# Hybrid attention/mLSTM block on one core: earlier parameter transposition, eight places for token tiles, row scales turned by VectorE, convolution in two halves

## The chip, the cores and the metric

One Trainium2 chip, one of its cores; one launch of one kernel. The metric is device time in microseconds (us) of that core. All engines of the core work side by side and meet at semaphores: TensorE (PE), VectorE (DVE), ScalarE (ACT), GpSimd (POOL), and SyncE (SP), which here only issues transfers.

## The reference, cut to what matters

Everything is float32. The input `x` is 1024 tokens by 1024 features. What bears on the change is the head of the block:

```python
h = rms_norm(x, g_mix[l])
p = h @ w_in[l]
aq, ak, av, mq, mk, mv, mo, mi, mf = jnp.split(p, split_idx, axis=-1)
...
qk = jax.nn.silu(causal_dwconv(jnp.concatenate([mq, mk], axis=-1), conv_qk[l]))
gates = jnp.concatenate([mi, mf], axis=-1).astype(jnp.float32) + b_gates[l].astype(jnp.float32)
...
mix = jnp.concatenate([rms_norm(att, g_attn_out[l]), rms_norm(mh, g_mlstm_out[l])], axis=-1)
x = x + mix @ w_out[l]
h2 = rms_norm(x, g_ffn[l])
x = x + (jax.nn.silu(h2 @ w_gate[l]) * (h2 @ w_up[l])) @ w_down[l]
```

`rms_norm` divides each token by the root of its mean square (the row scale) and multiplies by a gain per feature. `causal_dwconv` is a filter of four taps along the tokens on the 512 columns `mq, mk`. Windowed attention (eight heads) and a chunkwise mLSTM (four heads) stand between the two quoted pieces.

## The kernel before, in words

**Arithmetic.** Each float32 product is made of three matmuls of split operands: high by high, high by low, low by high (`three`, L829 to L835). A high part is written by ACT (`x_high`, `w0_high`, `w_high`) or, from the third weight group on, by POOL; the low part by DVE (`x_low`, `w0_low`) or POOL (`split`, L694).

**Order of the work.** Every engine runs a list that is written out by hand in its own block (`sync`, `gpsimd`, `tensor`, `scalar`, `vector`); what an engine's queue reaches late, everything behind it reaches late too.

1. `mq_half(0)` and `mq_half(1)` (L875 to L895) compute the 512 columns `mq, mk` in transposed form, features on partitions, for tokens 0 to 511 and 512 to 1023. Each half takes K = 8 blocks of 128 features, 12 matmuls each, into four banks: banks 0 to 3 in the first half, 4 to 7 in the second. `x_cols` is a transposed copy of x; its first half and the weights `w0_raw` come in as eight pairs of transfers (L556, L557), the second half as two transfers of 1 MB (`load_x_second`).
2. Units U = 8 to 55 (`unit`, then `out_unit`) work on one tile of 128 tokens each, eight units to a group (T = 8). Group 1 (U = 8 to 15) is 264 columns wide: keys, values and gates. Group 2 is the mLSTM values, 3 its output gate, 4 the queries, 5 and 6 the output projection. Units alternate between banks 0 and 1. Between the units small matmuls of the recurrence stand; the first of them, two products of `lf` with `tri` and `ones` (L1083, L1084), comes after unit U = 2T+2 = 18.
3. The feed-forward part: products of seven forms per quadrant from a fast 2 by 2 block scheme, with weight blocks streamed in by SP, split by ACT and POOL. It fills the time from about 380 us to the end and is not touched.

**Row scales.** They are not in the transposed product, so a scale per token is needed along the free axis. ACT squares and sums the eight token tiles `x_in` (`square_sum`, L1304), four at a time, and makes `rstd`, one column per tile (`row_scales`). `rstd` is stored to memory as a row of 512 numbers (`rstd_rows`), each of its elements a piece of its own, and SP loads that row into all partitions (`load_rstd`, L585). `mq_rows(b)` on DVE (L1710) multiplies half b by it on the way from the banks to `rawT`. Until `mq_rows(0)` has emptied two banks, unit U = 8 can't start (`mq_evac`). The four places of `x_in` are filled twice (`load_x`, L549).

**Parameters.** SP loads ten small pieces after the eight pairs (L558 to L568): the triangle `tri`, the rows of `prow` (convolution taps and gains), gate biases and sinks. PE transposes `prow` between the two halves (L1072) into bank 7; DVE copies the result to `cols` (L1813 to L1815) after all of its `x_low` work, and only then may PE write bank 7 again: `pe.wait_ge(gains_ready, 2)` stands before the fourth matmul of `mq_half(1)`.

**Convolution.** `convolution(f)` (L1774, L1776) handles 128 features by 1024 tokens in four passes of DVE; the four f run in U = 9 to 12 of DVE's list, after `mq_rows(1)`. ACT applies the SiLU to `qkT` f by f at U = 12, 14, 16 and 17 (L1451). Behind the convolution, DVE's list has U = 16: squares and sums of keys, gates (`absf`), and at U = 17 `lf` (L1857), which needs two small ACT steps (L1466, L1467) in between.

Of the kernel before, what the change touches and what calls it, by code (L numbers as in the profile page):

```python
# [29 lines left out]
ALU = mybir.AluOpType  # L30
# [43 lines left out]
def hymba_block(nc, x, g_mix, w_in, b_gates, conv_qk, q_gain, k_gain, sinks,  # L74
# [22 lines left out]
    x_t = x.rearrange("a (t p) d -> t p (a d)", p=P)  # L97
    out_t = out.rearrange("a (t p) d -> t p (a d)", p=P)
# [8 lines left out]
    with ctx:  # L107
# [64 lines left out]
        w0_raw, j_end = place("w0_raw", [P, K, N], at=J)  # L172
        ksq, _ = place("ksq", [P, T, P], at=J)
# [43 lines left out]
        grow, e = place("grow", [K, P], at=e)  # L217
        x_in = [x_in0, x_in1, x_in2, x_in3]
# [60 lines left out]
        rstd_s = sem("rstd_rows_loaded")  # L279
        w1_s = sem("w1_loaded")  # L280
# [264 lines left out]
        def _(sp):  # L545
            def load_x(t):
                if t >= 4:
                    sp.wait_ge(x_sq, t - 3)
                sp.dma_start(x_in[t % 4][:, :], x_t[t]).then_inc(x_in_s[t % 4], 16)  # L549
# [14 lines left out]
            for half in range(2):
                sp.dma_start(prow[G_K:G_K + 1, half * HD:(half + 1) * HD], k_gain).then_inc(par_s, 16)
                sp.dma_start(prow[G_Q:G_Q + 1, half * HD:(half + 1) * HD], q_gain).then_inc(par_s, 16)
            sp.dma_start(bias_g[:, :], b_gates[0:1, :].to_broadcast([P, 8])).then_inc(par_s, 16)
            sp.dma_start(sinks8[:, :], sinks[0:1, :].to_broadcast([P, 8])).then_inc(par_s, 16)  # L568
# [1662 lines left out]
```

## Time and profile before

| | |
|---|---|
| median of 3 runs | 1000.84 us (1000.76 to 1000.9) |
| profiled execution, its own time | 1005.44 us |
| its span | 1003.7 us |
| PE busy | 991.8 us (99%) |
| DVE, ACT, POOL busy | 635.1, 422.7, 668.4 us |
| moved by DMA | 70.69 MB |

The span is the stretch from the first to the last recorded instruction; the execution's own time holds it and a little around it. Busy time of PE counts matmuls with modelled ends, so 99% says that PE is almost always occupied, not how fast its clock runs; the granted clock (1.0 is full) stands in a column of its own in the view of stretches. A row of the timeline gives start, duration, engine, line, operation and tiles, and in brackets how long the engine had been idle and what ended that. SPq and ACTq are the queues that issue transfers.

### The profile page before, as it was taken

The page shows a single profiled execution, that of the slowest core. Times are in us where ns is not written, and L with a number is a line of the kernel's source. Part 1 is how long each engine was busy: PE and PEld are TensorE (multiplying, and loading weights), DVE is VectorE, ACT ScalarE, POOL GpSimd, SP SyncE. Part 2 cuts the span into 40 slices and gives each one's busy share as a digit, 9 for nine tenths or more (in the row PEclk, how much of TensorE's full clock was granted, in tenths as well). Part 3 has the DMA queues.
Part 4 walks back from the last instruction along what each step waited for, and adds up shares of the span by engine and source line. Part 5 has one row for each costly group of instructions (what it writes and reads, how often), then busy time and mean ns, then how long its engine had stood idle before and what let it go on. Part 6 is the DMA issues. An engine that isn't in the chain of part 4 may idle for free.

```text
span 1003.7 us, 13162 instructions
## 1 busy us (share of the span) xinstructions
PE 991.8 (99%) x4862; PEld 822.5 (82%) x4862; DVE 635.1 (63%) x777; ACT 422.7 (42%) x868; POOL 668.4 (67%) x529
## 2 busy tenths in 40 slices
PE   9899999999999999999999999999999999999998
PEld 7697788888888888888888888888888888888887
DVE  5259224558862677876748577774748586674585
ACT  6533135547750657524334352434334252433440
POOL 0238056726675516996887786887878788787792
PEclk9999999999999999999999999999999999999999
DMA  8823112141032002112112112112112112211213
GB/s 307 190 75 104 42 43 64 54 147 33 23 126 63 22 11 74 53 42 84 43 42 84 42 43 85 43 42 77 50 42 70 57 42 60 67 42 49 82 59 137
DMA packets 74423, 70.69 MB, mean 70 GB/s; under 512 B 6520, under 2 KB 54776, under 8 KB 74360
## 3 DMA queue, kind: packets, MB, share of 16 engines
q1 hardware_dynamic: 72296, 69.36, 22.6%
q10 hardware_dynamic: 2064, 0.50, 0.3%
q8 instruction: 39, 0.64, 0.3%
q14 instruction: 24, 0.20, 0.1%
HBM read 65.14 MB, written 4.21 MB: 69 GB/s over the span
## 4 chain that ended last, share of the span: by engine, by line
PE 87%; DVE 5%; DMA 3%; SPq 3%; ACT 1%; issue 1%; DVEq 0%; ACTq 0%
PE banks L833 27%; PE banks L835 27%; PE banks L834 27%; DVE qkT L1776 2%; DMA x_in<-in_x 1%; SPq L577 1%; DMA rstd_rows<-rstd 1%; PE banks L1030 1%; PE banks L846 1%; PE banks L927 1%; PE banks L1005 1%; DVE qkT L1774 1%; ACT prob L1541 1%; PE banks L992 1%; DMA rstd_b<-rstd_rows 1%
## 5 line engine op out<-in xcount | busy, mean ns | idle before, releaser
L763 POOL TENSOR_TENSOR wr_lo<-wr_raw,wr_hi 128x512 fp32r<-128x512 f32 x231 | 319.1, 1412 | 27.3 <-ACT wr_hi L1356 22.2
L757 POOL TENSOR_TENSOR wr_raw<-wr_raw,wr_raw 128x512 f32<-128x512 f32 x132 | 193.4, 1469 | 132.2 <-PE banks L835 75.8
L833 PE MATMUL banks<-hf_hi,wr_hi 128*128 128x512 f32 x616 | 240.2, 390 | 0.0
L835 PE MATMUL banks<-hf_hi,wr_lo 128*128 128x512 f32 x616 | 240.0, 390 | 0.0
L834 PE MATMUL banks<-hf_lo,wr_hi 128*128 128x512 f32 x616 | 239.9, 389 | 0.0
L1356 ACT ACTIVATE wr_hi<-wr_raw 128x512 fp32r<-128x512 f32 x231 | 136.7, 625 | 164.8 <-POOL wr_raw L757 107.7
L2177 DVE TENSOR_TENSOR x<-banks,x 128x1024 f32<-128x1024 f32 x138 | 168.8, 1224 | 51.5 <-PE banks L835 35.2
L833 PE MATMUL banks<-w_hi,actT_hi 128*128 128x512 f32 (+1 forms) x384 | 147.9, 385 | 0.0
L835 PE MATMUL banks<-w_hi,actT_lo 128*128 128x512 f32 (+1 forms) x384 | 144.2, 375 | 0.0
L834 PE MATMUL banks<-w_lo,actT_hi 128*128 128x512 f32 (+1 forms) x384 | 144.1, 375 | 0.0
L833 PEld LDWEIGHTS banks<-hf_hi,wr_hi 128*128 128x128 f32 x616 | 115.7, 188 | 24.3 <-issue 0.4
L835 PEld LDWEIGHTS banks<-hf_hi,wr_lo 128*128 128x128 f32 x616 | 115.7, 188 | 24.1
L834 PEld LDWEIGHTS banks<-hf_lo,wr_hi 128*128 128x128 f32 x616 | 115.7, 188 | 23.8
L833 PE MATMUL banks<-wr_hi,af_hi 128*128 128x512 f32 x308 | 120.0, 390 | 0.2 <-DVE x L2177 0.2
L834 PE MATMUL banks<-wr_lo,af_hi 128*128 128x512 f32 x308 | 120.0, 389 | 0.0
L835 PE MATMUL banks<-wr_hi,af_lo 128*128 128x512 f32 x300 | 116.8, 389 | 0.0
L2071 DVE TENSOR_TENSOR af_raw<-banks,af_raw 128x512 f32<-128x512 f32 x33 | 22.8, 691 | 128.9 <-PE banks L835 128.9
L694 POOL TENSOR_TENSOR w_lo<-w_raw,w_hi 128x512 fp32r<-128x512 f32 (+1 forms) x48 | 62.3, 1303 | 61.5 <-ACT w_hi L1372 58.9
L2095 DVE TENSOR_TENSOR af_lo<-af_raw,af_hi 128x512 fp32r<-128x512 f32 x75 | 88.8, 1226 | 0.3
L833 PEld LDWEIGHTS banks<-w_hi,actT_hi 128*128 128x128 f32 x384 | 72.9, 190 | 13.4 <-issue 1.4
L835 PEld LDWEIGHTS banks<-w_hi,actT_lo 128*128 128x128 f32 x384 | 72.8, 190 | 13.1
L834 PEld LDWEIGHTS banks<-w_lo,actT_hi 128*128 128x128 f32 x384 | 73.0, 190 | 11.6
(205 smaller groups left out, 1201.4 us busy)
## 6 DMA issues: line engine op xcount, KB each, us to landing
wr_raw<-in_w_up SPq DMA_DIRECT2D x46, 256.0 KB, 3.4
wr_raw<-in_w_gate SPq DMA_DIRECT2D x44, 256.0 KB, 3.3
wr_raw<-in_w_down SPq DMA_DIRECT2D x44, 256.0 KB, 3.2
w_raw<-in_w_in SPq DMA_DIRECT2D x32, 256.0 KB, 3.6
x_in<-in_x SPq DMA_DIRECT2D x8, 512.0 KB, 11.6
w_raw<-in_w_out SPq DMA_DIRECT2D x16, 256.0 KB, 2.6
x<-in_x SPq DMA_DIRECT2D x8, 512.0 KB, 5.6
out<-x SPq DMA_DIRECT2D x16, 256.0 KB, 2.1
```

The lines of the kernel that those rows point to most:

```text
L577: sp.dma_start(w1_raw[:, k, a:b], src).then_inc(w1_s, 16)
L694: nc.gpsimd.tensor_tensor(w_lo[:, ring, 0:width], w, w_hi[:, ring, 0:width].bitcast(F32), ALU.subtract).then_inc(w_ready, 1)
L757: nc.gpsimd.tensor_tensor(wr_raw[slot(q, f)][:, :], wr_raw[slot(q, a)][:, :], wr_raw[slot(q, b)][:, :], ALU.subtract).then_inc(wsum, 1)
L763: nc.gpsimd.tensor_tensor(wr_lo[s][:, :], wr_raw[s][:, :], wr_hi[s][:, :].bitcast(F32), ALU.subtract).then_inc(wf_lo, 1)
L833: nc.tensor.matmul(ps, x_hi, wh, start=first, stop=False, skip_group_check=more)
L834: nc.tensor.matmul(ps, x_hi, wl, start=False, stop=False, skip_group_check=more)
L835: return nc.tensor.matmul(ps, x_lo, wh, start=False, stop=last, skip_group_check=more)
L1356: nc.scalar.activation(wr_hi[s][:, :], wr_raw[s][:, :], ACT.Copy).then_inc(wf_hi, 1)
L1776: ins = V_.scalar_tensor_tensor(y, rawT[:, f, i:i + S], cols[:, 4 * i + f:4 * i + f + 1], y, ALU.mult, ALU.add)
L2071: V_.tensor_tensor(dst[:, :], src[:, :], dst[:, :], ALU.add).then_inc(added, 1)
L2095: V_.tensor_tensor(af_lo[b][f][:, :], af_raw[b][f][:, :], af_hi[b][f][:, :].bitcast(F32), ALU.subtract).then_inc(act_lo_s, 1)
L2177: V_.tensor_tensor(xs, banks[first + h][:, :, :], xs, ALU.add).then_inc(down_add, 1)
```

## The change

- The ten parameter loads of SP stand after the fourth of the eight pairs, not after the eighth.
- PE transposes `prow` inside `mq_half(0)`, before its block k = 6; DVE copies it to `cols` before its `x_low(1, k)` work.
- `x_in` has eight places (four tiles of two): the last four lie on `w0_raw`, which is dead once the first half's weights are split (`w0_ready`). Loads take two tiles each. The loads of `w1_raw` come after all of x, as two transfers in place of sixteen.
- DVE copies the four columns of `rstd` into a 32-wide tile and transposes it in blocks of 32 by 32 (`turn_scales`); ACT stores the turned rows in four transfers of four pieces of 128 bytes (`store_rows`) and ACT, not SP, loads the row back (`load_rows`).
- ACT's list: the squares of the second four tiles come before the splitting of group 1's weights, and `store_rows(1)` stands in the middle of the latter.
- The convolution is cut by tokens: 16 passes of 512 on the first half before `mq_rows(1)`, 16 on the second half after it, in place of 16 passes of 1024.

```diff
@@ layout
-        x_in0, e = place("x_in0", [P, D], at=E)
-        x_in1, e = place("x_in1", [P, D], at=e)
-        x_in2, e = place("x_in2", [P, D], at=e)
-        x_in3, e = place("x_in3", [P, D], at=e)
+        x_in0, e = place("x_in0", [P, 2, D], at=E)
+        x_in1, e = place("x_in1", [P, 2, D], at=e)
...
+        x_in2, _ = place("x_in2", [P, 2, D], at=J)
+        x_in3, _ = place("x_in3", [P, 2, D], at=J + 8 * D)
+        rpad, e = place("rpad", [P, 2, 32], at=e)
+        rpadT, e = place("rpadT", [P, 2, 32], at=e)
@@ sync
-            def load_x(t):
-                if t >= 4:
-                    sp.wait_ge(x_sq, t - 3)
-                sp.dma_start(x_in[t % 4][:, :], x_t[t]).then_inc(x_in_s[t % 4], 16)
+            def load_x(i):
+                sp.dma_start(x_in[i][:, :, :], x_p[:, 2 * i:2 * i + 2, :]).then_inc(x_in_s[i], 16)
...
-            for t in range(4):
-                load_x(t)
+            load_x(0)
+            load_x(1)
             load_x_second(1)
-            for k in range(K):
-                for (a, b), src in slice_source(k):
-                    sp.dma_start(w1_raw[:, k, a:b], src).then_inc(w1_s, 16)
-            for t in range(4, T):
-                load_x(t)
...
-            load_rstd(0)
+            sp.wait_ge(w0_ready, K)
+            load_x(2)
+            load_x(3)
+            sp.dma_start(w1_raw[:, :, 0:8], w_in_p[:, :, GATES:GATES + 8]).then_inc(w1_s, 16)
+            sp.dma_start(w1_raw[:, :, 8:NKV], w_in_p[:, :, AK:AK + 2 * KV * HD]).then_inc(w1_s, 16)
@@ tensor, mq_half
+                    if (b, k) == (0, 6):
+                        pe.wait_ge(gains_ready, 1)
+                        pe.wait_ge(par_s, 16 * PARAMS)
+                        nc.tensor.transpose(bank[7][:, 0:G_ROWS], prow[:, :],
+                                            ident[0:G_ROWS, 0:G_ROWS]).then_inc(gains_tp, 1)
@@ scalar
-                act.dma_start(rstd_dram[b:b + 1, :].rearrange("a (t p) -> p (a t)", p=P),
-                              rstd[:, tt], allow_slow_non_contiguous=True).then_inc(rows_stored, 16)
+            def store_rows(b):
+                act.wait_ge(rstd_turned, b + 1)
...
+                rows = rstd_dram[b:b + 1, :].rearrange("a (t q j) -> q (a t) j", q=4, j=32)
+                for q in range(4):
+                    act.dma_start(rows[q], rpadT[32 * q:32 * q + 4, b, :]).then_inc(rows_stored, 16)
+            def load_rows(b):
+                act.wait_ge(rows_stored, 16 * 4 * (b + 1))
+                act.dma_start(rstd_b[:, b * H:(b + 1) * H],
+                              rstd_dram[b:b + 1, :].to_broadcast([P, H])).then_inc(rstd_s, 16)
...
+            load_rows(0)
             for t in range(4, T):
                 square_sum(t)
             row_scales(1)
+            for n in range(4):
+                w_high(n)
+            store_rows(1)
+            for n in range(4, K):
+                w_high(n)
+            load_rows(1)
@@ vector
+            def turn_scales(b):
+                dve.wait_ge(rstd_ready, b + 1)
+                link(V_.tensor_copy(rpad[:, b, 0:4], rstd[:, 4 * b:4 * b + 4]))
+                V_.transpose(rpadT[:, b, :], rpad[:, b, :]).then_inc(rstd_turned, 1)
...
+            for k in range(4):
+                x_low(1, k)
+            turn_scales(0)
+            for k in range(4, K):
+                x_low(1, k)
             mq_rows(0)
+            dve.wait_ge(mq_evac, 4)
+            dve.wait_ge(x_sq, 4)
+            convolution(0, 0)
+            turn_scales(1)
+            for f in range(1, 4):
+                convolution(f, 0)
```

ACT's list from the first row scales on, before (L1315 is the store of `rstd`, L1326 `x_high`, L1372 `w_high`, L1304 a tile's squares):

```order
L1295 ACTIVATE rstd<-stat,cols 128x4
L1296 ACTIVATE rstd<-rstd 128x4
L1315 DMA rstd_rows<-rstd 128x4x1
L1326 ACTIVATE actT_hi<-actT_raw,cols 128x512 x4
L1372 ACTIVATE w_hi<-w_raw 128x264 x8
L1304 ACTIVATE junk,stat<-x_in_118 128x1024
L1304 ACTIVATE junk,stat<-x_in_119 128x1024
L1304 ACTIVATE junk,stat<-x_in_120 128x1024
L1304 ACTIVATE junk,stat<-x_in_121 128x1024
```

The same place of ACT's list now (L1312 is `store_rows`, L1316 `load_rows`, L1296 the squares, L1373 `w_high`):

```order
L1288 ACTIVATE rstd<-rstd 128x4
L1312 DMA rstd_rows<-rpadT 4x32 x4
L1327 ACTIVATE actT_hi<-actT_raw,cols 128x512 x4
L1316 DMA rstd_b<-rstd_rows 128x512
L1296 ACTIVATE junk,stat<-x_in_94 128x1024 x2
L1296 ACTIVATE junk,stat<-x_in_95 128x1024 x2
L1287 ACTIVATE rstd<-stat,cols 128x4
L1288 ACTIVATE rstd<-rstd 128x4
L1373 ACTIVATE w_hi<-w_raw 128x264 x4
L1312 DMA rstd_rows<-rpadT 4x32 x4
L1373 ACTIVATE w_hi<-w_raw 128x264 x4
L1316 DMA rstd_b<-rstd_rows 128x512
```

The squares moved ahead of the eight weight slices, and the second store now splits these slices four and four; each store waits for DVE's transposition, each load for the stores.

DVE's list from its second `x_low` series on, before (L1701 is `x_low`, L1813 and L1815 write `cols`, L1710 is `mq_rows`):

```order
L1701 SCALAR_TENSOR_TENSOR actT_lo<-actT_raw,cols,actT_hi 128x512 x8
L1813 COPY cols<-banks 128x26
L1815 TENSOR_SCALAR cols<-cols 128x1
L1823 COPY sink_b<-sinks_60 64x8 x2
L1825 TENSOR_SCALAR nsink<-sink_b 128x8
L1710 TENSOR_TENSOR rawT<-banks,rstd_b 128x512 x8
L1834 TENSOR_SCALAR nrstd<-rstd 128x8
L1837 MEMSET mvx 128x32
L1774 TENSOR_SCALAR qkT<-rawT,cols 128x1024
L1776 SCALAR_TENSOR_TENSOR qkT<-rawT,cols,qkT 128x1024 x3
```

DVE's list there now, from the copy to `cols` (L1824) on:

```order
L1824 COPY cols<-banks 128x26
L1826 TENSOR_SCALAR cols<-cols 128x1
L1834 COPY sink_b<-sinks_60 64x8 x2
L1836 TENSOR_SCALAR nsink<-sink_b 128x8
L1704 SCALAR_TENSOR_TENSOR actT_lo<-actT_raw,cols,actT_hi 128x512 x4
L1776 COPY rpad<-rstd 128x4
L1777 STREAM_TRANSPOSE rpadT<-rpad 128x32
L1704 SCALAR_TENSOR_TENSOR actT_lo<-actT_raw,cols,actT_hi 128x512 x4
L1713 TENSOR_TENSOR rawT<-banks,rstd_b 128x512 x4
L1782 TENSOR_SCALAR qkT<-rawT,cols 128x512
L1784 SCALAR_TENSOR_TENSOR qkT<-rawT,cols,qkT 128x512 x3
L1776 COPY rpad<-rstd 128x4
```

The copy to `cols` moved ahead of the eight `x_low`; `mq_rows` was one series of eight and is now four, the first convolution piece and the second turn, with the other pieces behind.

SP's list after the two large transfers of `x_cols`, before (L577 loads `w1_raw`, sixteen in all, of which the last two stand here; L549 is the second filling of `x_in`, L585 `load_rstd`):

```order
L577 DMA w_raw<-in_w_in 128x8
L577 DMA w_raw<-in_w_in 128x256
L549 DMA x_in_118<-in_x 128x1024
L549 DMA x_in_119<-in_x 128x1024
L549 DMA x_in_120<-in_x 128x1024
L549 DMA x_in_121<-in_x 128x1024
L585 DMA rstd_b<-rstd_rows 128x512
L613 DMA w_raw<-in_w_in 128x512 x2
L585 DMA rstd_b<-rstd_rows 128x512
L613 DMA w_raw<-in_w_in 128x512 x14
```

SP's list there now:

```order
L552 DMA x_in_120<-in_x 128x2x1024
L552 DMA x_in_121<-in_x 128x2x1024
L555 DMA actT_raw<-x_cols 128x4x512
L552 DMA x_in_94<-in_x 128x2x1024
L552 DMA x_in_95<-in_x 128x2x1024
L580 DMA w_raw<-in_w_in 128x8x8
L581 DMA w_raw<-in_w_in 128x8x256
L604 DMA w_raw<-in_w_in 128x512 x16
```

All of x is asked for before `w1_raw`, and neither load of the row scales is in SP's list any more.

## Rows read from the trace of the kernel before

**Rows 1.** Waits of PE: who for whom, us in total, times, longest.
```profile
PE banks L883 <- DVE cols L1815: 4.2, 1, 4.2
PE banks L1083 <- DVE lf L1857: 2.3, 1, 2.3
```

**Rows 2.** Timeline of PE around the two halves.
```profile
5.73 1.17 PE L883 MATMUL banks<-actT_hi,w_hi 128*128 128x512 f32 x4 [0.34 <-ACT w_hi L1360]
...
27.87 0.97 PE L883 MATMUL banks<-actT_hi,w_hi 128*128 128x512 f32 x3
33.03 0.80 PE L883 MATMUL banks<-actT_hi,w_hi 128*128 128x512 f32 x1 [4.19 <-DVE cols L1815]
...
54.71 1.07 PE L892 MATMUL banks<-actT_hi,w_lo 128*128 128x512 f32 x4
55.62 0.28 PE L833 MATMUL banks<-w_hi,actT_hi 128*128 128x264 f32 x1
```

**Rows 3.** Stretches with PE's busy time and granted clock, behind each long wait.
```profile
32.60:36.00 3.40, 2.97 (x7) 0.50 0.74 23
97.40:104.20 6.80, 6.73 (x18) 0.50 0.15 46
```

**Rows 4.** Timeline of PE around unit 19.
```profile
94.75 0.39 PE L835 MATMUL banks<-w_hi,actT_lo 128*128 128x512 f32 x1
97.47 0.64 PE L1083 MATMUL banks<-lf,tri 128*128 128x32 f32 x2 [2.33 <-DVE lf L1857]
...
98.35 0.78 PE L833 MATMUL banks<-w_hi,actT_hi 128*128 128x512 f32 x1
...
106.65 0.27 PE L1088 MATMUL banks<-ident,u 128*32 128x128 f32 x1
```

**Rows 5.** Timeline of DVE, 60 to 98 us.
```profile
60.74 2.48 DVE L1710 TENSOR_TENSOR rawT<-banks,rstd_b 128x512 f32<-128x512 f32 x4 [12.24 <-DMA rstd_b<-rstd_rows]
...
96.63 0.79 DVE L1857 SCALAR_TENSOR_TENSOR lf<-gate,expf 128x32 f32<-128x32 f32 x1 [0.56 <-ACT expf L1467]
```

**Rows 6.** Timeline of ACT, 20 to 97 us.
```profile
20.03 1.34 ACT L1326 ACTIVATE actT_hi<-actT_raw,cols 128x512 fp32r<-128x512 f32 x2 [3.33 <-DMA actT_raw<-x_cols]
...
28.21 0.40 ACTq L1315 DMA_DIRECT2D rstd_rows<-rstd  x1
...
89.74 0.69 ACT L1412 ACTIVATE mvx<-banks,rstd 128x512 f32<-128x512 f32 x1 [3.80 <-PE banks L835]
91.43 1.06 ACT L1451 ACTIVATE qkT<-qkT 128x1024 f32<-128x1024 f32 x1 [1.00 <-DVE qkT L1776]
92.51 1.28 ACT L1453 ACT_TABLE_LOAD   x1
94.92 0.31 ACT L1295 ACTIVATE krs<-kss,cols 128x16 f32<-128x16 f32 x1 [1.13 <-DVE kss L1847]
```

**Rows 7.** Timeline of SP's queue: issue of transfers.
```profile
9.13 0.45 SPq L558 DMA_DIRECT2D tri<-consts  x1
...
12.88 0.43 SPq L552 DMA_DIRECT2D actT_raw<-x_cols  x1
```

**Rows 8.** Stretches: ACT's busy time, PE clock, DMA share, GB/s.
```profile
14.00:17.00 3.00, 2.49 (x4) 1.00 0.56 117
...
30.00:39.00 9.00, 2.56 (x6) 0.81 1.03 68
```

**Rows 9.** Issues of transfers, 0 to 120 us: KB each, median us to landing.
```profile
rstd_rows<-rstd ACTq DMA_DIRECT2D x2, 2.0 KB, 9.0
nm_rows<-nM SPq DMA_DIRECT2D x1, 16.0 KB, 1.4
```

**Rows 10.** The row scales' way back into SBUF (`rstd_b`), both loads.
```profile
DMA to landing us min/median/max: 5.1/6.7/8.2
```

**Rows 11.** Timeline of POOL: the low parts of group 1's eight slices.
```profile
38.70 5.76 POOL L694 TENSOR_TENSOR w_lo<-w_raw,w_hi 128x264 fp32r<-128x264 f32 x8 [36.91 <-ACT w_hi L1372]
```

**Rows 12.** The line of the convolution on DVE: ns min/median/max.
```profile
L1776 DVE SCALAR_TENSOR_TENSOR qkT<-rawT,cols,qkT x12: 1284/1567/2415, 64.7 to 89.9; 128x1024 f32<-128x1024 f32 x12
```

More of the change, by code:

```diff
@@ L564, in _ @@
[L564 to L568, printed above, removed]
+                if k == 3:
+                    sp.dma_start(tri[:, :], consts[:, C_TRI:C_TRI + P]).then_inc(par_s, 16)
+                    sp.dma_start(prow[G_CONV:G_CONV + 16, :],
+                                 conv_qk.rearrange("a i (f p) -> (a i f) p", p=P)).then_inc(par_s, 16)
+                    for i, g in enumerate((g_att, g_ml)):
+                        rows = slice(G_OUT + 4 * i, G_OUT + 4 * i + 4)
+                        sp.dma_start(prow[rows, :], g.rearrange("a (k p) -> (a k) p", p=P)).then_inc(par_s, 16)
+                    for half in range(2):
+                        sp.dma_start(prow[G_K:G_K + 1, half * HD:(half + 1) * HD], k_gain).then_inc(par_s, 16)
+                        sp.dma_start(prow[G_Q:G_Q + 1, half * HD:(half + 1) * HD], q_gain).then_inc(par_s, 16)
+                    sp.dma_start(bias_g[:, :], b_gates[0:1, :].to_broadcast([P, 8])).then_inc(par_s, 16)
+                    sp.dma_start(sinks8[:, :], sinks[0:1, :].to_broadcast([P, 8])).then_inc(par_s, 16)
@@ L1069, in _ @@
             mq_half(0)
-            pe.wait_ge(gains_ready, 1)
-            pe.wait_ge(par_s, 16 * PARAMS)
-            nc.tensor.transpose(bank[7][:, 0:G_ROWS], prow[:, :],
-                                ident[0:G_ROWS, 0:G_ROWS]).then_inc(gains_tp, 1)
             mq_half(1)
@@ L1380, in _ @@
             act.wait_ge(ones_set, 2)
-            x_high(1, 0)
-            x_high(1, 1)
-            square_sum(0)
-            square_sum(1)
-            x_high(1, 2)
-            x_high(1, 3)
-            square_sum(2)
-            square_sum(3)
+            for k in range(4):
+                x_high(1, k)
+            for t in range(4):
+                square_sum(t)
             row_scales(0)
+            store_rows(0)
             for k in range(4, K):
                 x_high(1, k)
-            for n in range(K):
-                w_high(n)
+            load_rows(0)
             for t in range(4, T):
@@ L1767, in _, with convolution @@
                 w0_low(k)
[L1768 to L1774 removed]
+            def turn_scales(b):
+                dve.wait_ge(rstd_ready, b + 1)
+                link(V_.tensor_copy(rpad[:, b, 0:4], rstd[:, 4 * b:4 * b + 4]))
+                V_.transpose(rpadT[:, b, :], rpad[:, b, :]).then_inc(rstd_turned, 1)
+            def convolution(f, b):
+                y = qkT[:, f, b * H:(b + 1) * H]
+                link(V_.tensor_scalar(y, rawT[:, f, b * H:(b + 1) * H], cols[:, f:f + 1], None, ALU.mult))
                 for i in range(1, TAPS):
[L1776 to L1777 removed]
+                    ins = V_.scalar_tensor_tensor(y, rawT[:, f, b * H + i:b * H + i + H],
+                                                  cols[:, 4 * i + f:4 * i + f + 1], y, ALU.mult, ALU.add)
                     if i < TAPS - 1:
                         link(ins)
[L1780 removed]
+                    elif b == 0:
+                        step(ins)
+                    else:
+                        ins.then_inc(conv_ready, 1)
             def query_stats(t):
@@ L1838, in _ @@
                 if T + 1 <= U < T + 5:
-                    convolution(U - T - 1)
+                    convolution(U - T - 1, 1)
                 if U == 2 * T:
```

37 lines of the change are left out of this document (10 added, 27 removed).

## The prediction

> **What bounds the kernel now.** I read the busy table first: PE is busy 991.8 of 1003.7 us, so only what keeps PE waiting, or slows its clock, can be won. The waits of PE come next. Two stand out: 4.2 us for DVE's `cols`, 2.3 us for DVE's `lf` [rows 1]. The timeline shows what each cost.
>
> First seam. Four matmuls take 0.91 us (54.71 to 55.62). A half has 24 such fours, 21.8 us. The second half starts at 27.87, would end at 49.63 and ends at 55.62 [rows 2]. That is **6.0 us**: 4.5 of standing still (27.87 plus three matmuls is 28.55, the next one starts at 33.03) and 1.5 because the granted clock behind the wait is 0.50, the lower of the two levels, 1.2 GHz, until 36.0 [rows 3]. The missing thing is `gains_ready`: DVE copies `cols` behind its last four `x_low`, these need the last transfer of `x_cols`, and `cols` itself needs neither.
>
> Second seam. After the last matmul of unit 18 at 94.75 PE would go on at 94.98; it starts at 97.47, runs its two small products in 0.88 and unit 19 up to 106.65, and the clock is 0.50 for 6.8 us [rows 3, 4]. At the full clock the small ones take 0.44 and unit 19 takes 24 x 0.227 = 5.44, so PE would be through at 100.86: **5.8 us**. The chain of waits names the reason: row scales land, `mq_rows(1)` starts only at 60.74 after 12.2 us of idling, then come 27 us of convolution (passes from 64.7 to past 89.9) and 5 us of sums, and `lf` starts at 96.63 [rows 5, 12].
>
> Both waits are at the head. Behind unit 19 only waits of 0.4 us and less remain up to the last stage, and the later queues are paced by PE, so what the head saves moves everything forward.
>
> **The change, part by part.**
>
> *Parameters and `cols`.* The transposition moves from between the halves into the first, same cost. `gains_ready` comes about 1 us after PE's block 6, near 23 us, and PE asks for it at 28.5. The wait goes, with the low clock: -6.0. The price is SP's queue: ten issues between 9.13 and 12.88 [rows 7] now stand ahead of pairs 5 to 8, which are asked for 3.75 us later. Near 14 to 17 us the transfers dropped to 117 GB/s [rows 8]; I read that as these small pieces and move the hole to about 9 to 12. Pair 5 is then in near 13. PE needs block 4 at 5.73 + 4 x 2.72 = 16.6, and ACT at most 1.4 before that (two steps take 1.34 [rows 6]): 2 us of cover, and more for each later pair, since 2.72 us of PE stand against 1.3 of transfer. Cost nothing; if the cover is gone, PE waits for block 4. The large transfer behind keeps its place in the queue (issued at 12.88, in at 20.0 [rows 6, 7]). DVE's copies (0.9 us) delay its first `x_low(1, k)` to about 24; PE wants it at 28.8.
>
> *Row scales.* They are ready at 28.2, as before [rows 6]. Turning takes two small DVE operations, 0.5. Four issues of 0.4 end at 30.4. Then the store has to land. Before, 512 pieces of 4 bytes took 9.0 us; the only other store of rows, 32 pieces of 512 bytes, took 1.4 [rows 9]. Those are the bounds; for 16 pieces of 128 bytes I take 2, by the number of pieces, in which the new one is nearer to the fast row. ACT's four `x_high` (2.7) stand between, so `load_rows(0)` goes out at 33.1. It landed in 5.1 to 8.2 us before [rows 10]; the 8.2 fell into 30 to 39 us, where transfers crawled at 68 GB/s while the 4-byte pieces were under way [rows 8]. I take 5.1, so the scales are in at L = 38.4 (46.0 before). PE needs two banks emptied at 49.63: L + 1.3. Covered by 10 us.
>
> *The new queueing on ACT.* `store_rows(1)` waits for the second turn, which on DVE stands behind `mq_rows(0)` (2.5 us [rows 5]) and the first convolution piece. Behind the store on ACT are the last four slices of group 1's weights, and PE waits for those. A pass of 1024 took 1.28 to 2.42 [rows 12], so four passes of 512 cost 2.6 to 4.8; I take 3.2, since POOL is half idle there. Then 0.5 for the turn, 1.6 for the issues, and two slice steps of at most 0.72 each, ACT's and POOL's [rows 11]: slice 4 is ready at L + 9.2 = 47.6. PE wants it in unit 8 at 49.63 + 4 x 0.36 = 51.1 (264 columns of 512 make 0.12 a matmul). Cover 3.5. The second four squares (5.2 us from about 33 on, x being in without the crawl) are done by 39, ahead of that.
>
> By the Trainium skill, "SBUF — State Buffer", section "SBUF: two separate sides", an operation of DVE with two SBUF inputs and one of POOL that reads SBUF lock each other out for a whole instruction. The spread of [rows 12] agrees; four passes that each wait for one slice of 0.72 would leave 0.6 of the cover of 3.5, and the sum would be the same.
>
> *Convolution in halves.* 32 passes of 512 for 16 of 1024: the same elements. The first half's pieces now run while PE is in its second half. Row scales 1 are stored at 48.2, back at 53.4; pieces 1 to 3 end at 54.2; `mq_rows(1)` at 56.7; the second pieces at 70 (3.2 each) or 77 (4.8 each); DVE then waits for group 1, at 49.63 + 8 x 2.88 = 72.7. `absf` and the sums take some 5 us: ready by 78 to 82. PE asks for `lf` at 94.98 - 6.0 = 89.0. DVE is out of the way. Next latest is ACT, whose list is bound to PE. Behind unit 17, in old times: 89.74, 0.6 for the value tile, SiLU 1.1, table load 1.3, four small ones of 0.3, `lf` 0.8: 94.7 against 94.98 [rows 5, 6]. It fits by 0.3, less than one small DVE operation beside POOL. So -5.8, and I charge 0.3 for that chain.
>
> *The rest.* Two wide `w1_raw` loads for sixteen, behind x: needed by ACT at 39, in by 36. Eight tiles ask for no waiting on `x_sq`. Weights of groups 2 and 3 are paced by ACT's and POOL's lists per unit, thus by PE. Nothing.
>
> **Sum:** -6.0 - 5.8 + 0.3 = -11.5. The profiled execution took 1005.44, so 993.9 for one like it; it stands 4.6 above the median of the runs. From the median, 1000.84 - 11.5 = **989.3 us**.
>
> **The rivals.**
>
> 1. *The store lands halfway*, 5.5 us. L becomes 41.0 to 44.1 and slice 4 is late by 0 to 2.2; the second store holds ACT until 54.3 to 57.4, and unit 8 is emptied 1.1 later, while unit 10 wants its bank at 55.4: 0 to 3.1 more. With one fall of the clock like the first (1.5), about 4 us come back: 993.4. For: 128-byte pieces are still small. Against: 16 pieces.
> 2. *The second seam stays a short wait and the clock falls.* ACT's chain is late by 0.6, and 6.8 us at half clock cost 3.4 [rows 3]: 1000.84 - 11.8 + 4.0 = 993.0. For: the margin is 0.3. Against: the waits followed by a fall were 2.3 and 4.2 long, and the 0.34 at 5.73 was not.
> 3. *The small loads starve the first half.* Pair 5 lands 3.75 later than it must, less 2 of cover, and the clock falls: 1.8 + 1.5, 992.6.
> 4. *Slower: ACT hangs on its own stores.* If the store keeps its 9.0 us and the load its 8.2, L is 47.6 and slice 4 comes at 56.8, 5.7 late. The second store goes out by 55.4 and lands at 64.4; ACT stands in its queue until then, so unit 8's bank is free at 65.5 where unit 10 wants it at 61.1: 4.4. Two clock falls (1.5 and 3.4) make 15.0, more than the 11.8 won: 1004.0. It decides from about 8 us for a store. For: in the old order SP, not ACT, stood in this wait. Against: 1.4 us for 32 pieces [rows 9]. The Trainium skill, "DMA: Bandwidth & Descriptors", section "Specifications", says that transfers in pieces below 512 bytes make the DMA read, modify and write; turned rows stay below that, so by this rule the cost lies in the size as much as in the number, which speaks for this rival. No run here shows 128 bytes.
>
> **How the numbers follow.** Forecast 0.62, rival 1 0.15, rival 2 0.12, rival 3 0.06, rival 4 0.05. About 0.2% (2 us) is what a measurement of this kernel tells from no change. Only rival 4 is not faster: faster 0.94, same 0.02, slower 0.04. The range begins at 988.6 (both seams gone with nothing charged, 989.0, and some spread) and ends at 993.8, which takes in rivals 2 and 3 and the better half of rival 1.
>
> **What would show it.** Right: PE's wait for `cols` gone; unit 8 starts near 49.6 and group 2 near 72.7; granted clock 1.0 up to unit 19; `rstd_rows` in 1.4 to 3 us; `mq_rows(0)` near 38.4; no 68 GB/s stretch; PE's wait for `lf` at 0 to 0.5. Wrong: PE waiting in unit 8 for POOL's `w_lo`, in unit 10 for ACT's `kvs`, or in block 4 of the first half; a clock of 0.50 anywhere in the first 110 us; a store of 5 us or more.

## The result and the profile after

| | before | after |
|---|---|---|
| median of the runs, us | 1000.87 (1000.76 to 1001.13, 4 runs) | 995.63 (994.69 to 996.2, 4 runs) |
| ratio after / before | | 0.9941, 95% interval 0.9927 to 0.9955 |
| profiled execution: own time / span, us | 1005.44 / 1003.7 | 996.2 / 994.5 |
| mean granted clock of TensorE | 0.995 | 0.999 |

The change makes the kernel 5.2 us faster; 11.5 were forecast, and 995.63 lies above the range (988.6 to 993.8). Both waits at the head are gone all the same. The waits of PE in the changed kernel (who for whom, us in total, times, longest), against [rows 1]:

```profile
PE banks L1056 <- DVE cols L1762: 1.1, 1, 1.1
PE banks L879 <- ACT w_hi L1361: 0.6, 1, 0.6
PE banks L1026 <- ACT qT L1507: 0.4, 1, 0.4
PE banks L824 <- DVE x L2200: 0.2, 1, 0.2
```

The first two lie ahead of the first matmul of the projections, the others far behind unit 19. Stretches of the changed kernel (us, PE busy, granted clock, DMA share, GB/s), against [rows 3, 8]:

```profile
8.00:10.50 2.50, 2.50 (x8) 1.00 0.57 117
10.50:31.00 20.50, 20.50 (x91) 1.00 0.98 371
31.00:60.00 29.00, 29.00 (x160) 1.00 0.38 120
60.00:100.00 40.00, 40.00 (x245) 1.00 0.34 92
```

PE never stops in them, and no stretch at 0.50 is left. The timeline of PE in the changed kernel, against [rows 2, 4]:

```profile
6.01 2.05 PE L879 MATMUL banks<-actT_hi,w_hi 128*128 128x512 f32 x4 [0.62 <-ACT w_hi L1361]
7.86 1.91 PE L883 MATMUL banks<-actT_lo,w_hi 128*128 128x512 f32 x4
9.56 1.44 PE L888 MATMUL banks<-actT_hi,w_lo 128*128 128x512 f32 x4
10.84 1.09 PE L879 MATMUL banks<-actT_hi,w_hi 128*128 128x512 f32 x4
...
52.10 0.28 PE L824 MATMUL banks<-w_hi,actT_hi 128*128 128x264 f32 x1
...
97.39 0.27 PE L1080 MATMUL banks<-ident,u 128*32 128x128 f32 x1
```

Two things stand here. Unit 8 starts at 52.10 where 49.63 was worked out, and nearly all of the 2.5 us are lost at the start: 0.3 by a later first matmul, 2.1 up to 10.84, where the fours of matmuls take 1.85, 1.70 and 1.28 and 0.91 is the full pace. That is the pace of the lower level, 1.2 GHz: in e1 below, fours of the same shape take 1.70 and 1.71 where the granted clock is recorded as 0.50. Here it is recorded as 1.00. In [rows 2] the first four at 5.73 ran at full pace. Second, from unit 8 to the end of unit 19 (the transposition of `u`) PE takes 45.29 us, against 51.03 in the rows of before: that is the second seam, 5.7, gone.

DVE, ACT and POOL of the changed kernel, against [rows 5, 6, 11]; first DVE:

```profile
40.45 2.48 DVE L1713 TENSOR_TENSOR rawT<-banks,rstd_b 128x512 f32<-128x512 f32 x4 [5.06 <-DMA rstd_b<-rstd_rows]
...
47.03 0.21 DVE L1777 STREAM_TRANSPOSE rpadT<-rpad 128x32 f32<-128x32 f32 x1
...
58.94 2.48 DVE L1713 TENSOR_TENSOR rawT<-banks,rstd_b 128x512 f32<-128x512 f32 x4
...
90.14 0.19 DVE L1880 SCALAR_TENSOR_TENSOR lf<-gate,expf 128x32 f32<-128x32 f32 x1 [6.70 <-ACT expf L1470]
```

ACT, with its queue's issues (ACTq):

```profile
29.87 0.21 ACT L1288 ACTIVATE rstd<-rstd 128x4 f32<-128x4 f32 x1
30.55 1.29 ACTq L1312 DMA_DIRECT2D rstd_rows<-rpadT  x4
...
35.74 0.36 ACTq L1316 DMA_DIRECT2D rstd_b<-rstd_rows  x1
36.20 1.06 ACT L1296 ACTIVATE junk<-x_in 128x1024 f32<-128x1024 f32 x1 [1.74 <-DMA rstd_rows<-rpadT]
...
47.27 1.29 ACTq L1312 DMA_DIRECT2D rstd_rows<-rpadT  x4
...
49.45 0.35 ACTq L1316 DMA_DIRECT2D rstd_b<-rstd_rows  x1
...
86.22 0.69 ACT L1415 ACTIVATE mvx<-banks,rstd 128x512 f32<-128x512 f32 x1 [3.80 <-PE banks L826]
```

And POOL, the low parts of group 1:

```profile
42.04 3.54 POOL L685 TENSOR_TENSOR w_lo<-w_raw,w_hi 128x264 fp32r<-128x264 f32 x4 [40.25 <-ACT w_hi L1373]
49.11 5.68 POOL L685 TENSOR_TENSOR w_lo<-w_raw,w_hi 128x264 fp32r<-128x264 f32 x5 [3.53 <-ACT w_hi L1373]
```

`mq_rows(0)` starts at 40.45 (60.74 in [rows 5]), its second half at 58.94, and `lf` is written at 90.33, where PE asks for it at 91.46. So both waits went the way that was forecast. The two profiled executions differ by 9.2 us, the medians by 5.2: that was the question for the runs.

### The profile page after: what moved, and what is told of

It is laid out like the page before. It is cut to its first block, busy times and chain, and to the rows that moved or that the text cites. A ratio compares the mean times of both kernels' runs of the same rounds, so it can differ in the third digit from the quotient of the medians.

```text
span 994.5 us, 13172 instructions
## 1 busy us (share of the span) xinstructions
PE 988.7 (99%) x4862; PEld 820.4 (82%) x4862; DVE 640.2 (64%) x798; ACT 422.5 (42%) x868; POOL 666.5 (67%) x529
## 4 chain that ended last, share of the span: by engine, by line
PE 96%; DVE 2%; ACT 1%; issue 1%; DMA 0%; SPq 0%; DVEq 0%; ACTq 0%
PE banks L824 29%; PE banks L826 28%; PE banks L825 28%; PE banks L879 2%; PE banks L883 2%; PE banks L888 1%; PE banks L1026 1%; PE banks L837 1%; PE banks L923 1%; PE banks L1001 1%; ACT prob L1544 1%; PE banks L988 1%; PE banks L935 0%; PE banks L945 0%; DMA w_raw<-in_w_in 0%
```

## The experiments

A ledger of two times made all of them comparable. In every trace, of every kernel here, the stretch from the transposition of `u` (the end of unit 19) to the last instruction is 897.0 us within 0.2. So what a kernel is worth is decided by the time of that one row, and it splits at the start of unit 8. All in us, of each one's profiled execution:

| kernel | unit 8 starts | unit 8 to `u` | `u` | span | median |
|---|---|---|---|---|---|
| before, as in the rows | 55.62 | 51.03 | 106.65 | 1003.7 | 1000.87 |
| e1 before again | 56.76 | 45.29 | 102.05 | 999.1 | 1000.88 |
| e3 before, first half longer | 54.08 | 50.40 | 104.48 | 1001.5 | 1003.52 |
| e8 parameters alone | 52.27 | 54.04 | 106.31 | 1003.3 | 1004.89 |
| e11 all but the parameters | 60.22 | 45.29 | 105.51 | 1002.5 | 1003.71 |
| after, as above | 52.10 | 45.29 | 97.39 | 994.5 | 995.63 |
| e2 after again | 49.53 | 46.89 | 96.42 | 993.5 | 995.60 |
| e4 after, first half longer | 52.58 | 45.30 | 97.88 | 994.9 | 997.20 |
| e5 slices ahead of the store | 51.74 | 45.29 | 97.03 | 994.1 | 994.54 |
| e6 whole convolution | 50.53 | 45.30 | 95.83 | 992.8 | 995.15 |
| e7 pieces of 4 bytes | 49.46 | 54.02 | 103.48 | 1000.5 | 1002.33 |
| e9 e5 and wider filler | 50.08 | 45.29 | 95.37 | 992.3 | 994.36 |
| e10 e5 and longer filler | 50.82 | 45.29 | 96.11 | 993.1 | 993.95 |
| e12 longer filler alone | 49.84 | 46.66 | 96.50 | 993.5 | 995.21 |

45.29 is unit 8 to `u` with nothing in the way. The medians of e1 to e12 come from three chips: beside e1 to e4 the kernel before had a median of 1001.16, beside e5 to e8 1000.93, beside e9 to e11 1004.0 and beside e12 1003.89. The theory, in the form that it took after e1: the seams of before are in series against one chain on DVE, so an execution pays for one or for both, and the median one for less than the one in the rows. Its rivals: the change adds a wait of its own (the slices of unit 8 behind the store), or something far behind the head gives the rest back. The last of these falls with the 897.0.

**e1, the kernel before, unchanged.**

> The kernel before, once more. Theory A (the profiled execution of before was not a typical one: its two stretches at half clock behind the waits, 1.5 and 3.3 us, are missing in the timed runs, which stand 4.6 us below it): a fresh profile has a span near 999, the two waits of PE of 4 to 5 and 2 to 3 us, and no stretch at 0.50 behind them. Rival (the difference lies in something else of the profiled execution): span near 999 although both half-clock stretches are there, or a span near 1003.7 again. Time 1000.9.

1000.88 (1000.56 to 1005.45, 12 runs); ratio 0.9997 (0.9982 to 1.0012). Nine of its runs lie at 1000.6 to 1001.3 and three at 1003.8 to 1005.5, and now one of the nine was profiled. PE, e1:

```profile
28.87 0.97 PE L883 MATMUL banks<-actT_hi,w_hi 128*128 128x512 f32 x3
33.02 0.80 PE L883 MATMUL banks<-actT_hi,w_hi 128*128 128x512 f32 x1 [3.18 <-DVE cols L1815]
...
56.76 0.28 PE L833 MATMUL banks<-w_hi,actT_hi 128*128 128x264 f32 x1
...
96.12 0.30 PE L1083 MATMUL banks<-lf,tri 128*128 128x32 f32 x2
...
102.05 0.27 PE L1088 MATMUL banks<-ident,u 128*32 128x128 f32 x1
```

and the end of DVE's chain:

```profile
94.91 0.81 DVE L1857 SCALAR_TENSOR_TENSOR lf<-gate,expf 128x32 f32<-128x32 f32 x1 [0.56 <-ACT expf L1467]
```

Its clock behind the first seam (columns as above):

```profile
31.60:38.40 6.80, 5.38 (x13) 0.50 0.50 38
```

The execution near the median loses everything at the first seam: 1.0 at the start (the second half begins at 28.87, not 27.87), 3.5 of standing still, 2.65 of half clock (33.02 to 56.76 is 23.74, at full pace 21.09), together 7.1. PE then reaches `lf` at 96.12, when it is already there, and there is no second seam. In [rows 2 to 4] PE came to `lf` at 94.98, stood until 97.47, and the clock fell behind that too: 4.6 later, the 4.6 by which that execution stands above the median. Two things part the two executions: PE comes 1.1 later in e1, and `lf` is written 1.7 earlier (95.72 against 97.42), of which 0.4 is an earlier `mq_rows(1)` (60.32) and the rest a shorter convolution. In e1 `lf` is 0.4 ahead of PE. So of the 11.8 in the rows only 102.05 - 94.87 = **7.2** can be won from the median one (94.87 is 106.65 less 11.78). The expectation had both waits and no low clock, and the trace has one wait and a low clock, so of it only the span near 999 came true; neither did its rival come. That one seam is paid for was learned here. Open stays a third group of executions of before, at 1003.6 to 1004.5 with a mean clock of 0.997 (7 of 23 runs beside e5 to e8), which no trace here shows.

**e3 and e4, filler ahead of block 3 of the first half, in before and in after.** `keep_warm(n, w)` is n matmuls of ones, 128 times w columns wide, whose result nobody reads; one such filler, `keep_warm(4, 1)`, stands ahead of the first half in both kernels.

```diff
                 for k in range(K):
+                    if (b, k) == (0, 3):
+                        keep_warm(3, 4)
```

> Before, with three idle-purpose matmuls of ones (512 columns, float32) more in the first half, ahead of block 3; some 2.5 us of PE time more at full clock. Theory B: the wait for cols swallows them, PE resumes at 33.0 as before; time 1000.9 within 0.5. Rival (a loss at the start is paid in full in both kernels): 1003.4.

> The changed kernel with the same three matmuls more ahead of block 3. Theory B: nothing absorbs them; 995.5 + 2.5 = 998.0, and unit 8 starts 2.5 later. Rival: less than 1 us more.

e3: 1003.52 (1000.9 to 1005.75, 12 runs), ratio 1.0015 (1.0 to 1.003). The wait for `cols` vanished, since PE now comes to it at about 33, and with it the low clock; unit 8 started 2.7 us earlier than in e1. Then:

```profile
96.84 0.41 PE L1085 MATMUL banks<-lf,tri 128*128 128x32 f32 x2 [3.25 <-DVE lf L1859]
...
104.48 0.27 PE L1090 MATMUL banks<-ident,u 128*32 128x128 f32 x1
```

DVE finishes `lf` at 95.7 in e1 and at 96.8 here, though PE is 2.7 us further on here, so an early PE waits for it, and its clock falls. The 1000.9 expected left this out: the filler is swallowed by the first seam, and the second opens. This is the series connection, shown in one kernel. e4: 997.2 (996.1 to 999.12, 7 runs), 1.6 above after, where 998.0 was expected. Unit 8 starts at 52.58, 3.05 later than in e2: 0.44 is a later first matmul, 2.6 the filler in full, with no seam left to take it up. Why the median moved by 1.6 and not by 2.5, the next run explains.

**e2, the changed kernel, unchanged.**

> The changed kernel, once more. Theory B (its times, 994.7 to 996.2, spread because the clock's rise at the start falls at another moment in each execution, and no wait behind the first half absorbs it any more): times spread over 1 to 2.5 us, where those of before stay within 0.4; in the profile the first matmuls of the first half run at half clock for some microseconds, and unit 8 starts at 49.6 plus half of that stretch. Rival (the missing 2 us are a new wait): the profile shows a wait of PE of 1 us or more in the first 110 us.

995.6 (995.21 to 995.92, 6 runs), ratio 0.9939 (0.992 to 0.9959). PE, e2:

```profile
49.53 0.28 PE L824 MATMUL banks<-w_hi,actT_hi 128*128 128x264 f32 x1
...
52.34 0.39 PE L824 MATMUL banks<-w_hi,actT_hi 128*128 128x264 f32 x1 [0.26 <-POOL w_lo L685]
...
53.49 0.39 PE L824 MATMUL banks<-w_hi,actT_hi 128*128 128x264 f32 x1 [0.52 <-POOL w_lo L685]
...
96.42 0.27 PE L1080 MATMUL banks<-ident,u 128*32 128x128 f32 x1
```

Theory B's spread of 1 to 2.5 is not there (0.7), and the rival's wait of 1 us or more is not there in one piece either. Here the start runs at full pace, unit 8 begins on time, and now a wait shows that the first trace did not have: PE runs into the low parts of unit 8's last slices, and the way to `u` takes 46.89, not 45.29. POOL, e2 (a row of slices 4 to 7 and what follows, and the last slice's successor):

```profile
49.47 7.37 POOL L685 TENSOR_TENSOR w_lo<-w_raw,w_hi 128x264 fp32r<-128x264 f32 x6 [2.74 <-ACT w_hi L1373]
53.40 1.75 POOL L685 TENSOR_TENSOR w_lo<-w_raw,w_hi 128x512 fp32r<-128x512 f32 x1
```

The four slices go from 49.47 to 53.40, 0.98 each, where [rows 11] have 0.72. The last is wanted at 49.53 + 7 x 0.36 = 52.05. A late start, as in after, hides this wait, and this wait eats what an early start gains: two losses, 1.6 and 0 to 2.6 us, of which the larger counts. That is why unit-8 starts 2.6 apart (52.10, 49.53) leave spans 1.0 apart, and why e4's filler cost 1.6: it takes up the wait for the slices first. e5 and e12 test this.

**e5, all eight slices of group 1 ahead of the second store; e6, the convolution undivided; both from after.**

```diff
-            for n in range(4):
+            for n in range(K):
                 w_high(n)
             store_rows(1)
-            for n in range(4, K):
-                w_high(n)
```

> The changed kernel with all eight slices of group 1's weights split by ACT before it waits for the second turn of the row scales. Theory C (in executions whose clock is up early, unit 8 loses 1.6 us because slices 5 to 8 come after that wait and then one at a time from POOL beside the convolution; in executions with a late clock the loss is hidden): no wait of PE for w_lo, unit 9 starts 2.9 after unit 8; times 993.9 to 996 with a median of 994.6, 0.5 to 1.5 below the changed kernel. Rival (the loss in unit 8 is made good later, or the clock at the start decides all): 995.6, no change.

> The changed kernel with the convolution undivided, four f of four passes of 1024 behind mq_rows(1), as before; the second turn follows mq_rows(0) at once. Theory D (halving wins nothing: with row scales back early DVE is done in time either way, and the halves only take POOL's port while it splits the slices of unit 8): slices ready before 49, lf ready before PE asks at 89 to 90, no wait at the second seam; 994.6, like the kernel with the slices first. Rival (halving carries the second seam): DVE is late, PE waits 2 us or more for lf, the clock falls, 998 or more.

In e6 `turn_scales(1)` stands right behind `mq_rows(0)`, and `convolution(f)` runs whole in units 9 to 12, as before the change:

```diff
-            convolution(0, 0)
             turn_scales(1)
-            for f in range(1, 4):
-                convolution(f, 0)
...
-                    convolution(U - T - 1, 1)
+                    convolution(U - T - 1)
```

e5: 994.54 (994.0 to 995.89, 6 runs), ratio 0.9923 (0.9906 to 0.9939). e6: 995.15 (993.76 to 996.13, 6 runs), ratio 0.9927 (0.9911 to 0.9943). Both theories named 994.6. In neither trace does PE wait for `w_lo`, and behind unit 8 both take 45.3, so in them the start alone is left; the runs spread by 1.9 and 2.4 us, where e2's six lay within 0.7. POOL in e5:

```profile
42.44 7.47 POOL L685 TENSOR_TENSOR w_lo<-w_raw,w_hi 128x264 fp32r<-128x264 f32 x8 [40.65 <-ACT w_hi L1373]
```

and in e6:

```profile
42.63 5.88 POOL L685 TENSOR_TENSOR w_lo<-w_raw,w_hi 128x264 fp32r<-128x264 f32 x8 [40.84 <-ACT w_hi L1373]
```

The eight slices take 0.93 each beside convolution pieces and 0.74 where DVE has next to nothing to do. By the Trainium skill, "SBUF — State Buffer", section "SBUF: two separate sides", an operation of DVE with two SBUF inputs and one of POOL that reads SBUF hold one shared pair of ports in turn; these two rows agree in direction, at a quarter more for each slice; they don't show which engine held what. And e6 says what halving the convolution brings: nothing that the runs can tell. Undivided, it ends before PE needs it too (`lf` is written at 88.99, PE comes at 89.90).

**e7, the row scales stored from ACT in 512 pieces of 4 bytes, from after.**

```diff
-                for q in range(4):
-                    act.dma_start(rows[q], rpadT[32 * q:32 * q + 4, b, :]).then_inc(rows_stored, 16)
+                act.dma_start(rstd_dram[b:b + 1, :].rearrange("a (t p) -> p (a t)", p=P),
+                              rstd[:, 4 * b:4 * b + 4], allow_slow_non_contiguous=True).then_inc(rows_stored, 16)
```

> The changed kernel with the row scales stored as before, 512 pieces of 4 bytes per half, straight from the columns, but from ACT's new place and with the load on ACT's queue. By the fourth rival of the prediction: stores land in 8 to 10 us, row scales are in at 46 to 48, unit 8 waits 4 to 6 us for its slices, unit 10 again for ACT; about 1004. If the stores land in 5 us or less from there: 996 to 998.

1002.33 (1001.34 to 1004.54, 12 runs), ratio 1.0003 (0.9992 to 1.0015). ACT, e7:

```profile
30.75 0.41 ACTq L1311 DMA_DIRECT2D rstd_rows<-rstd  x1
41.57 0.34 ACTq L1316 DMA_DIRECT2D rstd_b<-rstd_rows  x1
42.02 1.06 ACT L1296 ACTIVATE junk<-x_in 128x1024 f32<-128x1024 f32 x1 [8.24 <-DMA rstd_rows<-rstd]
...
53.42 0.38 ACTq L1311 DMA_DIRECT2D rstd_rows<-rstd  x1
...
62.03 0.33 ACTq L1316 DMA_DIRECT2D rstd_b<-rstd_rows  x1
62.47 0.63 ACT L1373 ACTIVATE w_hi<-w_raw 128x512 fp32r<-128x512 f32 x1 [7.26 <-DMA rstd_rows<-rstd]
```

This is the first half of the slower rival: ACT hangs on its own stores, `mq_rows(0)` starts at 46.87, PE stands 4.4 us for `w_lo` in unit 8 and its clock falls. The other half, a wait in unit 10 for ACT, is not in the trace, and the 1004.0 at which the rival was priced was not reached. The turn to 16 pieces is worth 6.7 us in this arrangement, by the medians.

The second stores compare the two forms without other traffic. Stretches of ACT, first after, then e7 (columns: us, ACT busy, granted clock, DMA share, GB/s):

```profile
32.00:36.00 4.00, 2.46 (x4) 1.00 1.12 323
48.00:50.00 2.00, 1.37 (x4) 1.00 0.01 1
```

```profile
54.00:62.00 8.00, 1.21 (x4) 0.62 0.03 0
```

With the DMA engines nearly idle, the load goes out 0.9 us behind the last issue of 16 pieces (48.56 to 49.45) and 8.2 us behind the issue of 512 (53.80 to 62.03). The first stores went out beside the last of x: 3.9 and 10.4.

**e8, the parameters' part alone in before; e11, everything but it.**

```diff
+                if k == 3:
+                    sp.dma_start(tri[:, :], consts[:, C_TRI:C_TRI + P]).then_inc(par_s, 16)
...
+                    if (b, k) == (0, 6):
+                        pe.wait_ge(gains_ready, 1)
...
             V_.tensor_scalar(nsink[:, :], sink_b[:, :], -1.0, None, ALU.mult).then_inc(nsink_ready, 1)
+            for k in range(K):
+                x_low(1, k)
```

That was e8, from before. e11, from after, has the transposition between the halves again and `cols` behind all `x_low(1, k)`:

```diff
             mq_half(0)
+            pe.wait_ge(gains_ready, 1)
+            pe.wait_ge(par_s, 16 * PARAMS)
+            nc.tensor.transpose(bank[7][:, 0:G_ROWS], prow[:, :],
+                                ident[0:G_ROWS, 0:G_ROWS]).then_inc(gains_tp, 1)
             mq_half(1)
...
+            for k in range(4):
+                x_low(1, k)
+            turn_scales(0)
+            for k in range(4, K):
+                x_low(1, k)
             dve.wait_ge(gains_tp, 2)
```

> Before with the parameter part alone: loads after the fourth pair, transposition inside the first half, cols copied before x_low of the second half. Theory E (the two seams are in series against one clock, the chain of row scales and convolution on DVE, whose lf is ready near 96 to 97 whatever PE does): unit 8 starts at 49.6 to 52, then PE waits 5 to 8 us for lf at the second seam and the clock falls there: 1000.5 to 1002, no gain. Rival (each seam counts by itself): 995 to 997.

> The changed kernel with the parameter part taken back on PE and DVE: transposition between the halves, cols copied after all eight x_low of the second half; the loads stay early. Theory E (seams in series): PE waits for cols until about 36.3, the clock falls, unit 8 starts at 59 to 61, and with 942.3 us from there to the end the span is 1001.2 to 1003.3: time 1003 to 1005, slower than before, although the second seam is gone. Rival (each part is worth its own seam): 998 to 999.

e8: 1004.89 (1004.03 to 1007.26, 12 runs), ratio 1.0031 (1.0019 to 1.0043): **slower** than before. PE, e8:

```profile
52.27 0.28 PE L832 MATMUL banks<-w_hi,actT_hi 128*128 128x264 f32 x1
...
98.00 0.64 PE L1083 MATMUL banks<-lf,tri 128*128 128x32 f32 x2 [5.90 <-DVE lf L1857]
```

The wait for `cols` is gone, unit 8 starts 4.5 us earlier than in e1, and PE spends it and more standing for `lf`, 5.9 us, and the clock is at 0.50 when it goes on. The wait was as theory E had it; its time, 1000.5 to 1002, was 3 us too low. e11: 1003.71 (1002.89 to 1004.33, 12 runs), ratio 1.0004 (0.9992 to 1.0016); beside it the kernel before had 1004.0. The first seam has grown, as expected, and `lf` is in time:

```profile
36.53 0.80 PE L874 MATMUL banks<-actT_hi,w_hi 128*128 128x512 f32 x1 [7.05 <-DVE cols L1830]
...
60.22 0.28 PE L824 MATMUL banks<-w_hi,actT_hi 128*128 128x264 f32 x1
```

Either half of the change alone wins nothing; only together do they win.

**e9, e10 and e12, more filler ahead of the first matmul.** The loss that is left is the start at the lower pace. e12 is after, e10 is e5, each with this edit; e9 is e5 with `keep_warm(1, 4)` and `keep_warm(2, 1)` in its place:

```diff
-            keep_warm(4, 1)
+            keep_warm(6, 1)
```

> The kernel with the slices first, and another filler ahead of the first half: one matmul of ones of 512 columns and two of 128 in place of four of 128, some 0.6 us more of PE work, so that PE does not stand still before its first real matmul. Theory F (the clock comes up late, at up to 10.5 us, where PE's activity between 3 and 6 us was too thin): clock up by 8 us in the profile, times 993.8 to 995 with less spread, median 994.2. Rival (when the clock comes up is chance, whatever stands there): spread 994 to 996, median 994.5 to 995.

> The kernel with the slices first, with six fillers of 128 columns in place of four. Theory F by the gap alone (the standing still of 0.2 to 0.6 us ahead of the first real matmul is what makes the clock late): as above, 994.2. Rival (chance): no change against 994.5, or 0.3 more.

> The changed kernel with six fillers of 128 columns in place of four, and ACT's slices in the changed kernel's order. Theory G (the two losses hide each other: PE late from the start finds its slices ready, PE on time waits for them in unit 8, so the later of the two sets the end): with the clock up early PE waits 0.5 us or more for w_lo in unit 8 and behind unit 8 there are more than 942.3 us; median 995.0 to 995.7, no better than the changed kernel (995.6), while with the slices first the same fillers gave 994.0. Rival (the losses add, and the fillers take the start's share alone): 994.3 to 994.8 and no wait in unit 8.

e9: 994.36 (994.08 to 994.7, 5 runs), ratio 0.9907 (0.9891 to 0.9924). e10: **993.95** (993.66 to 994.99, 5 runs), ratio 0.9904 (0.9885 to 0.9923), the lowest median of all; its five runs lie at or below 994.99, those of the changed kernel at or above 994.69. e12: 995.21 (994.92 to 995.64, 6 runs), ratio 0.9921 (0.9902 to 0.9939). The kernel before had medians of 1004.0 and 1003.89 beside these three, as its executions of 1003.6 and more were the majority there, so their ratios flatter them and the times themselves are the thing to compare. e12 was on the same chip as e10, with the same filler; the slices' place is the only difference and is worth 1.3 us. PE's first four in e10 and in e4, and its wait in e12:

```profile
5.90 2.04 PE L879 MATMUL banks<-actT_hi,w_hi 128*128 128x512 f32 x4
```

```profile
5.94 1.17 PE L881 MATMUL banks<-actT_hi,w_hi 128*128 128x512 f32 x4 [0.82 <-ACT w_hi L1363]
```

```profile
53.37 0.39 PE L824 MATMUL banks<-w_hi,actT_hi 128*128 128x264 f32 x1 [0.52 <-POOL w_lo L685]
```

With the start early and the slices late, the wait is back (46.66 in the ledger), as theory G had it; the filler alone is worth 0.4 against after, within the spread. In these three traces unit 8 starts at 49.84 to 50.82, but in e2 and e7 it started at 49.53 and 49.46 with the old filler. The gap of theory F is not the cause: in e4 PE stood 0.82 us ahead of its first real matmul and ran at full pace from there, in e10 it stood not at all and the first four took 1.86. Whether more filler makes an early start likelier stays open, with one trace of each.

## Why the prediction was wrong

**First seam, -6.0: right.** The wait and the stretch at 0.50 are gone, and where the start runs at full pace unit 8 begins at 49.53 (49.63 worked out). The small loads cost PE nothing: ACT got block 4's pair at 14.02 (near 13 forecast, wanted before 15.2).

**Second seam, -5.8 + 0.3: right.** The chain behind unit 17 took from 86.22 to 90.33, 4.1 where 5.0 was worked out, so it fits by 1.1, and the 0.3 was not needed.

**The sum's anchor: this step failed.** "The profiled execution took 1005.44, so 993.9 for one like it; it stands 4.6 above the median of the runs. From the median, 1000.84 - 11.5." The 11.5 came out of a trace that paid for both seams; the execution near the median pays for one (e1). The 4.6 was itself part of the 11.5, and was taken off twice: 4.6 of the 6.3 by which 989.3 missed. Against the execution it was read from, the sum gives 993.9, and the changed kernel's runs are 994.7 to 996.2; the terms below are the rest. The sign was there before any run: 1005.44 lies far outside the 1000.76 to 1000.9 of the other three, so it could not be one of their kind. The mean granted clock tells them apart as well: 0.995 in that execution, 0.996 to 0.998 in the runs near 1001.

**"L = 38.4": 2.0 too early.** (The terms as written add up to 38.2.) `mq_rows(0)` started at 40.45. The row scales are ready at 30.1, not at 28.2 "as before". The ten small loads ahead of `x` are half of that: with them alone (e8) it is 29.0, against 28.2 in e1. For the rest the trace has ACT standing 1.36 us for a transfer of `x_in` before the third tile's squares; the tiles now come in pairs. Then the store: ACT's four `x_high` ended at 34.46, and ACT stood until the store let the load go at 35.74. So it landed 3.9 us behind the last issue, while the DMA engines were full, where 2 was taken "by the number of pieces"; the second store of the same form took at most 0.9. With the form held, what else was under way makes the difference of 3.0. The issues and the load were together 0.7 shorter. The load's upper bound of 8.2 was also misread: that load ran from 37.81 to 46.01, behind the 4-byte pieces and not beside them.

**"Cover 3.5" for the slices: wrong term.** It was taken at the first of the four slices (47.6 against 51.1). But POOL makes one in 0.72 and PE uses one up in 0.36, so the last decides: 49.8 forecast, by the same numbers, against 52.1 wanted, a cover of 2.3. In e2 it came at 53.40, 3.6 late: 2.4 from L, 0.2 from the steps between, 1.0 from slices of 0.98. That is the wait for `w_lo` which the text named as a sign of being wrong, and it costs 1.6.

One more sum does not come out: with 4.8 for every piece the second half of the convolution ends at 82, not at 77. That is still ahead of the 89.0 at which PE asks.

**The start: not in the sum at all.** The first matmuls ran at full pace in [rows 2], so their pace was taken as given. It varies: in e2, e4, e7 and e12 the first real four runs at full pace, in after and e8 full pace comes only between 10 and 11 us, and unit 8 starts 0 to 2.6 late. In before the first seam hid this, as the restart hangs on DVE and came at 33.03 and 33.02 in both traces. With the seam gone it shows.

The books: 7.2 to be won from the median execution, less 1.6 for the slices or up to 2.6 for the start, whichever is larger, leaves 4.6 to 5.6 against an execution like e1. Measured: 5.2.

**The rivals.** None of the four came. The first had its mechanism half right (scales late, unit 8's slices late) but its bank wait in unit 10 is in no trace. The second and third left no row: no wait for `lf`, no low clock, no wait in block 4. The fourth needs the 4-byte pieces, and came by half with them (e7). The Trainium skill's rule on pieces below 512 bytes ("DMA: Bandwidth & Descriptors", section "Specifications") spoke for it. Both stores here are below that size. Of the 512 pieces of 4 bytes the load came 8.2 and 10.4 us behind the issue, of the 16 pieces of 128 bytes 0.9 to 4.2 (after, e2, e11). So being under that bound decided nothing here; between the two forms number and size changed together, and which of them did it stays open.

## What to carry to other kernels

Before terms are subtracted from a median, ask whether the profiled execution is a median one: where it stands apart, find which of its waits the others lack, and count that one only once. Price waits that end on the same chain together, not each by itself: an engine that arrives earlier at the first waits longer at the next, and half of a change can be a loss where the whole is a gain. Where a producer is slower per piece than its consumer, work out the cover at the last piece, and when a wait is removed, look for what it had been hiding, back to the first instruction.

## What the runs showed of the hardware

- TensorE's first matmuls ran at half pace (fours in 1.85 and 1.70 us) for 4.8 us behind the filler in the changed kernel's first trace (5.0 in e8), in some executions and not in others of the same kernel, while the granted clock of those stretches is recorded as 1.00 and the mean of the changed kernel's runs as 0.999 to 1.000. Only the durations show it.
- The clock fell to 0.50 (1.2 GHz) with the waits of 3.2 us (e1, e3), 3.6 (e7), 5.9 (e8) and 7.1 (e11): in e3 and e7 1.5 and 0.7 us after PE had gone on, in e1, e8 and e11 while it still stood. No low clock is recorded behind the 0.26 and 0.52 of e2.
- POOL's 264-column subtractions took 0.93 to 0.98 us beside DVE's convolution pieces (e5, e2) and 0.74 us beside an idle DVE (e6), and DVE's 512-column passes spread from 0.75 to 1.77 us.
- One and the same store, 16 pieces of 128 bytes in four issues, let the load behind it go 3.9 us after the last issue with the DMA engines full (share 1.12, 323 GB/s) and 0.9 us after it with them idle (share 0.01).
